# Main matmuls with a step of -1 on the moving operand and on the PSUM output

## What is computed

```python
h = rms_norm(x, ln_mix_w)
u_pool, q, f_logit, inp, g, gate_a, gate_b = split(h @ w_in)          # 2048 x 9216
y_a = multiscale_pool(u_pool, pool_mix_w, pool_scale) @ w_branch_a    # 1024 x 2048
y_b = hgrn2(q, f_logit, inp, g, lb, hgrn_norm_w) @ w_branch_b         # 1024 x 2048
x = x + (sigmoid(gate_a) * y_a + sigmoid(gate_b) * y_b) @ w_out       # 2048 x 2048
u_gate, u_val = split(causal_depthwise_conv(rms_norm(x, ln_ffn_w) @ w_up, conv_w, conv_b))  # 2048 x 11008
x = x + (silu(u_gate) * u_val) @ w_down                               # 5504 x 2048
x = x + sigmoid(rms_norm(x, ln_ple_w) @ w_ple_gate) * (p @ w_ple)     # 2048 x 2048, 256 x 2048
out = rms_norm(x, ln_final_w)
```

## Time and profile before

| what | value |
|---|---|
| median of three runs (lowest, highest) | 1490.14 us (1489.63, 1490.71) |
| time of the profiled execution | 1489.77 us |
| its span, from the first to the last instruction | 1488.0 us |
| TensorE matmul busy, share of the span | 1460.8 us, 98% |
| TensorE weight load busy | 1219.2 us, 82% |
| VectorE busy | 872.0 us, 59% |
| ScalarE busy | 747.4 us, 50% |
| mean granted TensorE clock | 0.997 |

### The profile page before, as it was taken

The page is one execution under the profiler, slowest core; times in us unless marked ns, Lnnn a source line. Parts: engine busy times, 40 slices in busy tenths (PEclk is TensorE's granted clock), DMA queues, the critical chain, the costliest instruction groups (busy, mean ns, idle before and its releaser), DMA issues.

```text
span 1488.0 us, 18747 instructions
## 1 busy us (share of the span) xinstructions
PE 1460.8 (98%) x6814; PEld 1219.2 (82%) x6814; DVE 872.0 (59%) x968; ACT 747.4 (50%) x918; POOL 125.8 (8%) x80
## 2 busy tenths in 40 slices
PE   7999999999999999999999999999999999999996
PEld 5888888888888888888888888888888888888884
DVE  4576676445454545556676676666666455454554
ACT  5555645444444444545555555555555444344543
POOL 1034143100000000001010010110110000000000
PEclk9999999999999999999999999999999999999998
DMA  6744455455565655565655656556555555555652
GB/s 234 253 149 149 156 156 156 141 166 188 193 189 193 188 195 185 186 184 174 197 183 180 196 178 189 184 180 194 183 155 191 207 194 193 184 198 182 222 192 91
DMA packets 189466, 271.88 MB, mean 183 GB/s; under 512 B 11348, under 2 KB 103080, under 8 KB 189280
## 3 DMA queue, kind: packets, MB, share of 16 engines
q1 hardware_dynamic: 189120, 270.88, 55.8%
q0 software_dynamic: 288, 0.21, 0.0%
HBM read 268.95 MB, written 2.10 MB: 182 GB/s over the span
## 4 chain that ended last, share of the span: by engine, by line
PE 90%; issue 7%; DVE 1%; ACT 1%; DMA 0%; POOL 0%; POOLq 0%; ACTq 0%; SPq 0%; DVEq 0%
PE main L521 28%; PE main L523 28%; PE main L522 28%; PE aux L538 3%; PE aux L585 2%; PE aux L619 0%; DVE w_lo L946 0%; DMA x_tok<-in_x 0%; PE aux L609 0%; DVE cv L1089 0%; ACT w_hi L742 0%; DVE bT L1046 0%; POOL dec L1242 0%; ACT cv L850 0%; PE aux L598 0%
## 5 line engine op out<-in xcount | busy, mean ns | idle before, releaser
L946 DVE TENSOR_TENSOR w_lo<-raw,w_hi 128x1024 fp32r<-128x1024 f32 x508 | 651.6, 1287 | 549.9 <-ACT w_hi L742 548.7
L742 ACT ACTIVATE w_hi<-raw 128x1024 fp32r<-128x1024 f32 x508 | 535.9, 1056 | 644.0 <-PE main L523 629.4
L521 PE MATMUL main<-w_hi,xT_hi 128*128 128x512 f32 (+1 forms) x1408 | 552.1, 392 | 4.3 <-DVE w_lo L946 4.3
L523 PE MATMUL main<-w_hi,xT_lo 128*128 128x512 f32 (+1 forms) x1408 | 546.4, 388 | 0.0
L522 PE MATMUL main<-w_lo,xT_hi 128*128 128x512 f32 (+1 forms) x1408 | 546.3, 388 | 0.0
L521 PEld LDWEIGHTS main<-w_hi,xT_hi 128*128 128x128 f32 x1408 | 265.2, 188 | 57.8 <-issue 4.4
L523 PEld LDWEIGHTS main<-w_hi,xT_lo 128*128 128x128 f32 x1408 | 265.1, 188 | 54.0
L522 PEld LDWEIGHTS main<-w_lo,xT_hi 128*128 128x128 f32 x1408 | 265.4, 188 | 51.9
L521 PE MATMUL main<-w_hi,aT_hi 128*128 128x512 f32 x344 | 134.6, 391 | 0.1
L523 PE MATMUL main<-w_hi,aT_lo 128*128 128x512 f32 x344 | 134.1, 390 | 0.0
L522 PE MATMUL main<-w_lo,aT_hi 128*128 128x512 f32 x344 | 134.1, 390 | 0.0
(11 more groups left out here) (157 smaller groups left out, 916.3 us busy)
## 6 DMA issues: line engine op xcount, KB each, us to landing
raw<-in_w_up SPq DMA_DIRECT2D x336, 256.0 KB
raw<-in_w_in SPq DMA_DIRECT2D x144, 512.0 KB
raw<-in_w_down SPq DMA_DIRECT2D x84, 512.0 KB
raw<-in_w_out SPq DMA_DIRECT2D x32, 512.0 KB
raw<-in_w_ple_gate SPq DMA_DIRECT2D x32, 512.0 KB
raw<-in_w_branch_a SPq DMA_DIRECT2D x16, 512.0 KB
raw<-in_w_branch_b SPq DMA_DIRECT2D x16, 512.0 KB
x_tok<-in_x SPq DMA_DIRECT2D x4, 512.0 KB, 8.0
```

Of the source, the lines that this page charges most:

```text
L521: pe.matmul(acc, th, wh, start=first, stop=False)
L523: mm = pe.matmul(acc, tl, wh, start=False, stop=end)
L742: ac.activation(w_hi[:, u % RING, :, 0:w], raw[:, u % RING, :, 0:w], ACT.Copy).then_inc(hi_full, 1)
L946: dve.tensor_tensor(w_lo[:, u % RING, :, 0:w], raw[:, u % RING, :, 0:w], w_hi[:, u % RING, :, 0:w].bitcast(F32), ALU.subtract).then_inc(lo ...
```

## The change

The three access patterns of the 6072 main matmuls that run along the 512 (or 256) columns are turned round: the two moving operands and the accumulator. The first column that enters the array is now column 511, and the first result goes to column 511 of the bank, so each product lands where it did. In memory, each of these patterns now starts at its last element and has a step of -1 element (4 bytes back) where it had 1. The stationary operand keeps its pattern, and so do all the other instructions, on all engines; the number and the order of the instructions are the same.

```diff
@@ -512,11 +512,11 @@
                 pe.wait_ge(lo_full, plus(u + 1, 2 * UK, it))
                 for a in range(tiles):
                     for tb in range(TB):
-                        acc = main_acc(c, tb, width)
+                        acc = main_acc(c, tb, width)[:, ::-1]
                         th = hi[:, k + a, tb * P:(tb + 1) * P]
                         tl = lo[:, k + a, tb * P:(tb + 1) * P]
-                        wh = w_hi[:, u % RING, a, 0:width]
-                        wl = w_lo[:, u % RING, a, 0:width]
+                        wh = w_hi[:, u % RING, a, 0:width][:, ::-1]
+                        wl = w_lo[:, u % RING, a, 0:width][:, ::-1]
                         first, end = i == 0 and a == 0, i == n - 1 and a == tiles - 1
                         pe.matmul(acc, th, wh, start=first, stop=False)
                         pe.matmul(acc, th, wl, start=False, stop=False)
```

## The result

| | before | after |
|---|---|---|
| median, us | 1489.89 (4 runs, 1489.35 to 1490.71) | 1526.6 (4 runs, 1526.39 to 1526.77) |
| ratio, 95% interval | | 1.0246 [1.0228, 1.0264] |
| span of the profiled execution, us | 1488.0 | 1524.8 |
| mean granted TensorE clock | 0.997 | 0.997 |

The account below looks back on a forecast made before the run. TensorE's main-matmul pace was taken to bound the kernel. The profiled execution's 1489.77 us plus 0 for every part, with the median of three runs 0.4 us more, gave 1490.1 us; range 1487 to 2700 us.

Parts of the forecast that it names:

- What bounds the kernel: TensorE, busy 1460.8 of 1488.0 us: time is main matmuls times their pace, plus side work, head and tail.
- Dependencies: Matmuls adding into one bank are all turned together, so each accumulator column is touched again after 0.2267 us as before; cost nothing.
- weight loads: The stationary operand keeps its pattern; its loads stay busy for 1219.2 us beside the matmuls; cost nothing.
- writing of PSUM: Main matmuls' accumulator stream, bounded together with the moving operand's reading between 81 us less and 3752 us more; taken as 0.
- I take 0 us: Value chosen for turned moving-operand reads and PSUM writes in main matmuls: same consecutive elements, last first, no gap.
- The row that I let decide: Score matmuls of 64 columns: step 2 took 1.71 us against 1.70 for whole runs, at most 1.66 ns per column.
- The 13.3 ns: Part of each main matmul's 0.2267 us left after 512 columns at 0.4167 ns; 81 us over 6072 matmuls.
- Half rate: Rival: a turned main-matmul stream fails to pair elements, 0.427 us per 512 columns; 1204 us more, 2694 us; chance 0.22.
- A dearer start of each matmul: Rival: turned patterns cost at their ends, 6.07 us per ns; 13.3 ns doubled gives 1571 us; chance 0.10, shared.
- a partial slowing between none and half rate: Rival: main matmuls slow by less than a drop to 1.2 GHz column pace; no size of its own; shared chance 0.10.
- Faster: Rival: the 13.3 ns per main matmul go, 81 us less, 1409 us; chance 0.03.
- that rival of the forecast: The build puts the main matmuls' patterns back in order and runs the old kernel; same time, within the 0.60 chance.

Follow-up runs that it names:

- output_only: Kernel before the change with only the PSUM output written from column 511 down, moving operand read upwards: 1489.61 us, ratio 1.0.
- moving_only: Kernel before the change with only the two moving operands read from column 511 down, PSUM written upwards: 1526.77 us, ratio 1.0246.
- EO: Chunk walk in a variant of the kernel before: moving operand read in even columns, then odd, PSUM written upwards; 454.3 ns between starts at 512 columns.
- i4: Kernel before with moving operand and PSUM in ascending blocks of 4 columns, each walked downwards: 1489.66 us, ratio 0.9999.
- I16: Kernel before with moving operand and PSUM in ascending blocks of 16 columns, each walked downwards: 266.6 ns in one chunk; whole kernel 1724.09 us, ratio 1.1573.

## Why the prediction was wrong

The forecast was no change, 1490.1 us; the changed kernel takes 1526.6 us.

**What bounds the kernel: right.** TensorE's pace is the time; all 36.7 us came through the distance of starts, and nothing else moved.

**Dependencies, weight loads, writing of PSUM at nothing: right.** `output_only` measured the write by itself, 1489.61 us, and the loads are busy for 1220.2 us against 1219.2.

**The step that failed** is "I take 0 us. A turned stream touches the same consecutive elements in the same consecutive pairs and quadruples". Reading the moving operand downwards costs 6.7 ns at 512 columns, 36.9 us in `moving_only`. Two things in it were mistaken. The row that I let decide shows a stream that has up to 1.66 ns per column; it could bound the cost but say nothing on the value at 0.42 ns, where a step of 2 costs 227 ns per matmul (EO), though it cost nothing there. And within 16 bytes the argument is true (`i4`: 1489.66 us), but I carried it over to the order of the larger pieces, which I didn't look at.

**The 13.3 ns "that has nothing to do with the columns"** was a difference of two widths read as a constant. It is 11.2 to 16.8 ns upwards over 16 widths, depends on where both operands begin, and is 2.5 ns with bf16. No row ahead of the runs could tell it from a fixed cost of each matmul.

**The rivals.** Half rate did not come with a contiguous walk of either sign; it is what EO, a step of 2, does (454.3 ns). "A dearer start of each matmul" had about the right size by its price of 6.07 us per ns (6.7 ns give 40 us, against 36.7, since narrow units, neighbours of side work and slow distances don't pay), and its doubled gap was an upper figure. Its mechanism is not what the runs show: the test that I had named for it, the same ns at 512 and at 256 columns, gave +6.7 and -1.3. Its chance of 0.10 was shared with a partial slowing between none and half rate, and a partial slowing is what happened. "Faster", for which I knew of no mechanism, came in the units of 256 columns alone, by 1.1 ns. The reversal was really made, since the distances moved: that rival of the forecast is out.

**What stays open.** Why the order matters. The runs bound it: the read side, pieces of 16 to 128 bytes in downward order, at 4 bytes per column, at 2.4 GHz, clearly so in matmuls of 384 columns and more, and not as a price of one matmul. The weight load's part is open as well: its length makes no difference with bf16, but place, width and spacing of the stationary operand move the distances of float32r by up to 6.7 ns. The distances of the three plain cases at 512 columns are multiples of 6.67 ns, the time of 16 columns or 64 bytes: 34 of them upwards (226.7), 35 downwards (233.3), 40 for I16 (266.7), which is the walk that turns round within 64 bytes. Other means (230.0, 231.6, 234.5, 236.6) are no such multiples. Two streams that are served in turns of that length would fit the three, but that is a guess, and no run isolates such a thing.

## What to carry to other kernels

Before a pattern of the moving operand is called free, ask how many bytes per column it passes over: with 2 the order of a contiguous walk was free here, with 4 it was not. Then keep it ascending in runs of at least 64 float32, and leave no gaps between the elements. The direction in which PSUM is written is free in this kernel, so a reversal that is needed belongs on the output, or within 16 bytes. A row whose instruction is bound by something else tells an upper bound for a cost, and never that the cost is zero.

## What the runs showed of the hardware that I had not expected

- Walking 16-column blocks downwards is the worst contiguous walk of those tried: 266.7 ns against 233.3 for the full reversal, 15.7% on the whole kernel.
- A float32r moving operand at a step of 2 elements takes twice the time, 454.3 against 226.9 ns; with bf16 the same step costs 10 ns, 225.9 against 215.9.
- At 256 columns the downward read is the faster one (118.4 against 119.5 ns, chunk means of the two kernels at the end of w_up).
- Turning some of the matmuls can cost more than turning all: 234.5 against 233.3 ns (two lines of three, or the first token block of two).
- Fewer contiguous stationary columns make an upward float32r matmul slower, 226.7 ns at 128 and 230.0 to 231.6 at 96, 64 and 32; 64 of them at step 2 don't (226.7).
